# A hybrid decoder layer on one core: who finishes the last gate tiles, and the order of the work around them

## What is computed

```python
mixed = jnp.concatenate([rms_norm(attn_out, attn_out_g[i]),
                         rms_norm(gmlp_out, gmlp_out_g[i])], axis=-1)
...
gate = jax.nn.sigmoid(jnp.einsum('bsd,de->bse', h, w_ple_gate[i]) + b_ple_gate[i])
ple = jnp.einsum('bsp,pd->bsd', p[i], w_ple[i]) * gate
h = h + rms_norm(ple, ple_post_g[i])
```

## Time and profile before

| | |
|---|---|
| time of the kernel before, three runs | 576.51, 577.04, 576.51 us, median 576.51 |
| the profiled execution's own time | 577.25 us |
| its span, first to last instruction | 575.5 us |
| TensorE busy | 566.9 us (99%) |
| VectorE busy | 504.1 us (88%) |
| ScalarE busy | 380.1 us (66%) |
| GpSimd busy | 96.5 us (17%) |

### The profile page before, as it was taken

How to read it: one execution, slowest core, us unless ns; L and a number is a source line. 1 busy time by engine, 2 the same in 40 slices (tenths; PEclk the granted TensorE clock), 3 DMA queues, 4 the chain that set the end, 5 groups by cost and what they waited for, 6 DMA issues and landing times.

```text
span 575.5 us, 8898 instructions
## 1 busy us (share of the span) xinstructions
PE 566.9 (99%) x3348; PEld 494.6 (86%) x3348; DVE 504.1 (88%) x661; ACT 380.1 (66%) x603; POOL 96.5 (17%) x159
## 2 busy tenths in 40 slices
PE   9999999999999999999999999999999999999994
PEld 8888888888888888999899999999899999988884
DVE  5799986788866988999989989999999898798898
ACT  6896774777656746656566575764666565686784
POOL 0321437000103401101010010011010100015122
PEclk9999999999999999999999999999999999999999
DMA  8982008313103597377476393583773754897933
GB/s 260 328 330 112 0 2 322 117 47 102 38 1 110 196 330 205 75 232 180 73 263 132 77 278 85 161 241 52 247 164 86 245 124 97 305 231 165 236 118 148
DMA packets 28603, 93.73 MB, mean 163 GB/s; under 512 B 3216, under 2 KB 4624, under 8 KB 28304
## 3 DMA queue, kind: packets, MB, share of 16 engines
q1 hardware_dynamic: 20736, 67.64, 33.1%
q0 software_dynamic: 5328, 19.14, 19.1%
q10 hardware_dynamic: 2496, 6.37, 3.1%
HBM read 86.85 MB, written 6.29 MB: 162 GB/s over the span
## 4 chain that ended last, share of the span: by engine, by line
PE 90%; DVE 4%; DMA 2%; ACT 1%; issue 1%; POOL 1%; DVEq 0%; ACTq 0%; POOLq 0%
PE psum L2760 28%; PE psum L2764 28%; PE psum L2765 28%; DMA raw_second<-weights_dram 2%; PE psum L2991 2%; PE psum L2971 2%; PE psum L2815 2%; DVE w_lo L1404 1%; PE psum L2860 1%; DVE h L1514 1%; PE psum L2829 1%; DVE psum L1491 1%; ACT junk_late L1652 0%; DVE actT_lo L1460 0%; POOL stat L2404 0%
## 5 line engine op out<-in xcount | busy, mean ns | idle before, releaser
L2760 PE MATMUL psum<-t_hi,a_hi 128*128 128x512 f32 x216 | 84.7, 392 | 0.0
L2764 PE MATMUL psum<-t_lo,a_hi 128*128 128x512 f32 x216 | 84.6, 392 | 0.0
L2765 PE MATMUL psum<-t_hi,a_lo 128*128 128x512 f32 x216 | 84.0, 389 | 0.0
L2760 PE MATMUL psum<-w_hi,actT_hi 128*128 128x512 f32 (+1 forms) x178 | 69.7, 392 | 0.0
L2765 PE MATMUL psum<-w_hi,actT_lo 128*128 128x512 f32 (+1 forms) x178 | 68.6, 385 | 0.0
L2764 PE MATMUL psum<-w_lo,actT_hi 128*128 128x512 f32 (+1 forms) x178 | 68.5, 385 | 0.0
L2765 PE MATMUL psum<-sum_hi,up_lo 128*128 128x256 f32 x224 | 63.4, 283 | 0.0
L2764 PE MATMUL psum<-sum_lo,up_hi 128*128 128x256 f32 x224 | 63.4, 283 | 0.0
L2760 PE MATMUL psum<-sum_hi,up_hi 128*128 128x256 f32 x224 | 63.2, 282 | 0.0
L2765 PE MATMUL psum<-actT_hi,up_lo 128*128 128x256 f32 (+1 forms) x200 | 60.0, 300 | 0.0
L2764 PE MATMUL psum<-actT_lo,up_hi 128*128 128x256 f32 (+1 forms) x200 | 60.0, 300 | 0.0
(11 more groups left out here) (291 smaller groups left out, 1469.7 us busy)
## 6 DMA issues: line engine op xcount, KB each, us to landing
raw<-weights_dram SPq DMA_DIRECT2D x39, 512.0 KB, 4.3
raw_o<-weights_dram SPq DMA_DIRECT2D x23, 512.0 KB, 4.9
raw_x<-weights_dram POOLq DMA_DIRECT2D x21, 512.0 KB, 5.5
raw_second<-weights_dram SPq DMA_DIRECT2D x16, 512.0 KB, 4.0
raw_x<-weights_dram SPq DMA_DIRECT2D x9, 512.0 KB, 6.1
qk_raw<-weights_dram SPq DMA_DIRECT2D x8, 512.0 KB, 7.5
raw_o<-weights_dram POOLq DMA_DIRECT2D x7, 512.0 KB, 6.8
raw_second<-weights_dram POOLq DMA_DIRECT2D x6, 512.0 KB, 8.0
```

Of the source, the lines that this page charges most:

```text
L2760: begin = nc.tensor.matmul(out, a_hi, b_hi, start=first, stop=False, skip_group_check=read_between)
L2764: nc.tensor.matmul(out, a_hi, b_lo, start=False, stop=False, skip_group_check=read_between)
L2765: return nc.tensor.matmul(out, a_lo, b_hi, start=False, stop=last, skip_group_check=read_between)
```

## The change

Nothing is computed differently; some steps go to another engine, some change their place in a queue.

1. Tile 6's norm weight: `GAINED_BY_POOL` is now (0, 1, 6). Gate and product of tile 6 are kept in SBUF (`acc`) instead of PSUM, `gain_by_pool(6)` runs on GpSimd between rstd(0) and rstd(3), and add(6) reads `ple_late_b` in SBUF.
2. Tile 7's last step: ScalarE multiplies by the root into `ple_late_a` (`scale_gained`, 128x256), and GpSimd adds h (`add_by_pool`, 128x256). VectorE no longer has add(7).
3. Orders: VectorE's and ScalarE's lists at the end, and the order of the stores (now 2, 3, 0, 5, 4, 6, 8, 7, 1; for tile 7 SyncE waits for GpSimd).
4. In attention, `attn_scale(2)` stands ahead of `drain_pt0(7)` on VectorE, and `turn_scale(2)` ahead of `turn_probs(7)` on TensorE.

```diff
-GAINED_BY_POOL = (0, 1)
+GAINED_BY_POOL = (0, 1, 6)
+GAINED = (2, 3, 4, 5, 7, 8)
+SCALED_BY_ACT = 7
...
-            return acc[:, t, 0:W] if i < 2 else gate_result(i)
+            return acc[:, t, 0:W] if i in GAINED_BY_POOL else gate_result(i)
...
+        def scaled_of(i):
+
+            t, c0, width = GATE_TILES[i]
+            return ple_of(t)[:, c0:c0 + width]
...
             scale_probs(8)
             attn_spread(2)
+            attn_scale(2)
             drain_pt0(7)
-            attn_scale(2)
             drain_pt0(8)
...
-            GAINED = (2, 3, 4, 5, 6, 7, 8)
...
             gate_fold(1)
+            gate_ple(3)
+            gate_c22(1)
             gain_ple(2)
-            gate_c22(1)
-            gate_ple(3)
             gate_ple(4)
             gain_ple(3)
+            add_ple(2)
+            gate_ple(5)
+            add_ple(3)
             gain_ple(4)
-            gate_ple(5)
-            add_ple(2)
-            add_ple(3)
             gain_ple(5)
             gate_ple(6)
             add_ple(0)
             gate_ple(7)
             add_ple(5)
-            gain_ple(6)
+            gain_ple(7)
             gate_ple(8)
-            gain_ple(7)
             add_ple(4)
+            add_ple(6)
             gain_ple(8)
-            add_ple(6)
+            add_ple(8)
             add_ple(1)
-            add_ple(7)
-            add_ple(8)
...
+            def scale_gained(i):
+                t, c0, width = GATE_TILES[i]
+                act.wait_ge(pl_rstd, TOKENS_DONE.index(t) + 1)
+                act.wait_ge(pl_gained, GAINED.index(i) + 1)
+                nc.scalar.activation(scaled_of(i), gained_of(i), ACT.Copy, scale=rstd_pl[:, t:t + 1]
+                                     ).then_inc(c_copied, 1)
...
             square_ple(1)
+            sigmoid(3)
             square_ple(2)
-            sigmoid(3)
+            square_ple(3)
             sigmoid(4)
-            square_ple(3)
             square_ple(4)
             sigmoid(5)
             square_ple(5)
             sigmoid(6)
             sigmoid(7)
             square_ple(6)
+            square_ple(7)
             sigmoid(8)
-            square_ple(7)
             square_ple(8)
+            scale_gained(SCALED_BY_ACT)
...
+            def add_by_pool(i):
+                t, c0, width = GATE_TILES[i]
+                cut = slice(c0, c0 + width)
+                pool.wait_ge(c_copied, 3 * LAST + len(GATE_COPIES) + 1)
+                nc.gpsimd.tensor_tensor(h[:, t, cut], scaled_of(i), h[:, t, cut], ALU.add
+                                        ).then_inc(gained_by_pool, 1)
...
             ple_rstd(0)
+            gain_by_pool(6)
             ple_rstd(3)
             partial_sum(7)
             ple_rstd(1)
+            add_by_pool(SCALED_BY_ACT)
...
-            order = (2, 3, 0, 5, 4, 6, 1, 7, 8)
...
+            order = (2, 3, 0, 5, 4, 6, 8, 7, 1)
+            added_by_dve = [i for i in order if i != SCALED_BY_ACT]
...
             proj(23, range(3, 7))
+            turn_scale(2)
             turn_probs(7)
-            turn_scale(2)
             turn_probs(8)
```

More of the change, by code:

```diff
@@ L2741, in _ @@
             sp.dma_start(ple_late[1][:], ple_spill[:, 2:4, :]).then_inc(ple_loaded[1], 16)
-            order = (2, 3, 0, 5, 4, 6, 1, 7, 8)
-            for n, i in enumerate(order):
+            order = (2, 3, 0, 5, 4, 6, 8, 7, 1)
+            added_by_dve = [i for i in order if i != SCALED_BY_ACT]
+            for i in order:
                 t, c0, width = GATE_TILES[i]
-                sp.wait_ge(out_ready, n + 1)
+                if i == SCALED_BY_ACT:
+                    sp.wait_ge(gained_by_pool, len(GAINED_BY_POOL) + 1)
+                else:
+                    sp.wait_ge(out_ready, added_by_dve.index(i) + 1)
                 sp.dma_start(out[t * P:(t + 1) * P, c0:c0 + width], h[:, t, c0:c0 + width]
```

## The result

The changed kernel takes 577.61 us (median of 22 runs, 577.28 to 578.23), the kernel before in the same runs 576.60 (576.26 to 577.13): a ratio of 1.0016, 95% interval 1.0010 to 1.0022, so 1.0 us slower. The forecast was 576.7 with a range to 577.4: the direction was right, the size was not, and the result lies above the range. The profiled execution of the changed kernel has 577.63 us and a span of 575.8.

The account below looks back on a forecast made before the run. TensorE, busy 566.9 of 575.5 us, was taken as the bound, leaving its standstills and the tail behind its last matmul. Tail +0.4 and middle -0.18 gave 0.2 us slower: 576.51 + 0.2 = 576.7 us, range 575.8 to 577.4.

Parts of the forecast that it names:

- The middle: Attention, units 7 and 8: attend(7) begins 0.18 us earlier (bounds 0 and 0.27), carried to the end in full.
- Steps 1 to 6: The tail: GpSimd's tile 6 pass, root and tile 7 addition, held by add(0), add(6), add(1), end at 568.41, 571.21, 572.98.
- held root: Tail, step 5: rstd(1)'s second operation, 0.11 us behind add(6), is held to 570.78 and ends at 571.21.
- Step 7: Tail's end: SyncE issues tile 7's store, then add(1)'s at 573.5 against 573.1 before, so the tail grows by 0.4 us.
- The carrying to the median: Whole kernel: the profiled execution lies 0.74 us above the median, so the 0.2 difference is added to 576.51, giving 576.7.
- The range: Whole kernel: 575.8 to 577.4 us, taking in the forecast with its variants and the rival with GpSimd ahead of add(1).
- The rivals: At the end: GpSimd comes first, 575.85 us, chance 0.25; GpSimd holds VectorE at add(0), 577.85 us, chance 0.07.
- GpSimd was not first: Rival at the end: root escapes add(6), GpSimd's addition precedes add(1), last store 0.45 us earlier; 575.85 us, chance 0.25.

Follow-up runs that it names:

- e3: The changed kernel with tile 7's last step back on VectorE, as an addition between tile 8's and tile 1's: 576.62 us, ratio 1.0007 to the kernel before.
- e4: The changed kernel with tile 6's norm weight back on VectorE, tile 7 still finished by ScalarE and GpSimd: 577.70 us, ratio 1.0024 to the kernel before.
- e5: The changed kernel with tile 7's last step back on VectorE and add(6) moved behind gain(8): 576.23 us, ratio 0.9991 to the kernel before.

## Why the prediction was wrong

- **The middle**: right. 0.18 was forecast and 0.18 came at attend(7), held by ScalarE's drain as forecast; 0.17 of it was still there 300 matmuls later.
- **Steps 1 to 6**: right, collision by collision, each within 0.1 us if counted from the last matmul. Root to the end of GpSimd's addition was forecast at 1.77 us (571.21 to 572.98) and was 1.76 (570.71 to 572.47). The multiply took 0.47 (forecast 0.37) behind a hop of 0.04 (forecast 0.08). Only the weight given to the held root was wrong as far as add(8) is concerned: that addition would have waited for gain(8) until 570.74 instead of 570.75 with the root unheld (estimated as for e3).
- **Step 7, the first that failed**: the sum ended at the landing of the last store, and what GpSimd does behind its last operation was put at nothing. The last store was well placed: 5.63 after the start of the last matmul was forecast (573.5 less 567.87), 5.49 came. (VectorE itself was done at 571.89; tile 1's store waited in SyncE's queue behind tile 7's, issued at 572.50.) But GpSimd, now the last worker, has its DRAIN of 3.1 us behind it, and that ended 0.42 after SyncE's. None of the rows shown told of it; the records did, where GpSimd's DRAIN ended only 0.86 us ahead of SyncE's before the change. Moving GpSimd's end from 571.18 to 572.98, as forecast, should have raised the question.
- **The carrying to the median, the second**: the forecast took the profiled execution's tail of 7.35 as the kernel before's, and its 0.74 us above the median as something that both kernels share. It was not shared. The tail to SyncE's DRAIN was 7.44 in that execution and 7.07 in two others; the changed kernel has 7.78, and e4, with a transfer as late as that of before, 7.83. So the late transfer goes with an old tail that is 0.37 longer, and seems to lengthen the new one hardly (two profiles of different kernels, and the changed kernel's has a wait of 0.31 for it), and the loss against an ordinary execution of before is 0.71, not the 0.34 that the profile shows (0.4 was forecast).
- **The sum with the measured terms**: -0.17 (middle) + 0.71 (stores) + 0.42 (DRAIN) + 0.02 (barrier) = 0.98, against a difference of the medians of 1.01. The two failed terms are 0.37 and 0.42 of it. The profiles also differ by up to 0.2 us ahead of the middle, where nothing was changed, so the agreement to 0.03 is partly luck.
- **The range**: its upper end does not come out of its own terms; 576.51 + 0.95 - 0.18 is 577.3 and not 577.4. The result lies above both. And 0.2% is not the least that can be told: the measured interval is 0.06% to either side.
- **The rivals**: neither came. GpSimd was not first (add(6) was 0.13 ahead of the root, 0.11 was forecast), and no VectorE addition at the end took more than 0.75.

## What to carry to other kernels

An engine's last instruction is not its end: read the records behind it before a step is given to an engine that used to finish early, and count its closing time against that of the stores. When a wait is taken away, look for the one that ends next, before the gain is put down to it: in e3 the two were 0.01 us apart. Give a slow helper steps in the middle of its queue, not the last one; on tile 5 the same kind of step did not set the end. And before a profiled execution is carried to the median, ask which of its waits an ordinary execution does not have.

## What was not expected of the hardware

GpSimd's closing DRAIN lasts 3.087 us from its issue behind the finished last operation in every profile where it is not issued earlier, whether that operation was 0.22 or 0.57 long and whichever it was; VectorE's and ScalarE's end 0.03 to 0.05 us after their last operation. And a held GpSimd operation loses 0.14 us less than the time for which VectorE's operation still ran, whatever its width: the root 0.47 of 0.61 (1.04 for 0.57), the addition of tile 7 0.39 of 0.53 (1.11 for 0.72) and 0.52 of 0.66 in e4 (1.24), the norm weight 0.38 of 0.52 (1.67 for 1.29). The other way round, with the root issued 0.20 ahead, neither lost anything that the rows show (e5).
